# Three attention mixers on TensorE: the value products of the batch before, then the transposes of this batch

## What is computed

```python
s = jnp.einsum('bqhd,bkhd->bhqk', qb, k) * scale
q_pos = i * Q_BLOCK + jnp.arange(Q_BLOCK)
p = masked_softmax(s, key_pos[None, :] <= q_pos[:, None])
return jnp.einsum('bhqk,bkhd->bqhd', p.astype(v.dtype), v)
```

## Time and profile before

| what | us |
|---|---|
| median of 3 executions | 2275.53 |
| lowest and highest of them | 2273.96 and 2278.75 |
| the profiled execution | 2274.43 |
| its span, first to last instruction | 2272.6 |
| of it PE busy | 2130.4 (94%) |
| first attention, about | 152 to 176 |
| MLA's attention, about | 1478 to 1503 |
| NSA's attention, about | 1990 to 2057 |

### The profile page before, as it was taken

One profiled execution on the slowest core, in us unless ns is written; L12 is line 12 of the kernel. 1 busy time (PEld: TensorE's weight loads), 2 busy tenths in 40 slices (PEclk: granted clock), 3 DMA queues, 4 the chain that ended last, 5 costly groups with the idle time before them and its releaser, 6 DMA issues.

```text
span 2272.6 us, 26953 instructions
## 1 busy us (share of the span) xinstructions
PE 2130.4 (94%) x10954; PEld 1282.6 (56%) x10954; DVE 1031.1 (45%) x1712; ACT 673.4 (30%) x1055; POOL 25.4 (1%) x38
## 2 busy tenths in 40 slices
PE   5999899998999899899968999999999999989998
PEld 3348743333333234333315887778888886567887
DVE  7986712222222122222216555765555553375555
ACT  3144311111011011001004444564444442165443
POOL 0000000000000000000000000100000000200000
PEclk8999899999999999999988999999999999989999
DMA  7773799999999999999996452344553443313441
GB/s 317 295 279 125 275 408 426 427 428 427 427 426 428 428 427 427 428 427 426 426 426 258 178 210 92 149 167 167 206 211 139 184 186 116 148 57 137 196 180 70
DMA packets 43506, 633.83 MB, mean 279 GB/s; under 512 B 5104, under 2 KB 5104, under 8 KB 6288
## 3 DMA queue, kind: packets, MB, share of 16 engines
q1 hardware_dynamic: 43376, 632.04, 67.7%
HBM read 630.97 MB, written 1.05 MB: 278 GB/s over the span
## 4 chain that ended last, share of the span: by engine, by line
PE 73%; DMA 15%; DVE 7%; ACT 3%; issue 2%; SPq 0%; ACTq 0%; DVEq 0%
DMA piece<-in_moe 15%; PE bank L2407 13%; PE bank L2302 12%; PE bank L2304 12%; PE bank L2303 12%; PE bank L2448 6%; PE bank L643 3%; PE bank L2388 2%; PE bank L2472 2%; PE bank L1059 1%; PE bank L2748 1%; PE bank L2784 1%; ACT ffn_hi L2909 1%; PE bank L1235 1%; DVE ffn_lo L2308 1%
## 5 line engine op out<-in xcount | busy, mean ns | idle before, releaser
L2407 PE MATMUL bank<-piece,xeT 128*64 128x512 f32 (+1 forms) x2304 | 447.9, 620 | 50.5 <-DMA piece<-in_moe 42.6
L2308 DVE TENSOR_TENSOR ffn_lo<-slot,ffn_hi 128x2048 fp32r<-128x2048 f32 x132 | 302.0, 2291 | 153.2 <-ACT ffn_hi L2909 147.6
L2407 PEld LDWEIGHTS bank<-piece,xeT 128*64 128x64 f32 (+1 forms) x2304 | 135.0, 131 | 330.1 <-issue 307.0
L2909 ACT ACTIVATE ffn_hi<-slot 128x2048 fp32r<-128x2048 f32 x132 | 251.8, 1913 | 126.3 <-PE bank L2304 115.9
L2302 PE MATMUL bank<-ffn_hi,hT_hi 128*128 128x512 f32 x672 | 265.4, 395 | 2.8 <-DVE ffn_lo L2308 2.8
L2304 PE MATMUL bank<-ffn_hi,hT_lo 128*128 128x512 f32 x672 | 261.9, 390 | 0.0
L2303 PE MATMUL bank<-ffn_lo,hT_hi 128*128 128x512 f32 x672 | 261.4, 389 | 0.0
L2527 DVE TENSOR_TENSOR hT<-hT,bank 128x512 f32<-128x512 f32 x144 | 92.1, 681 | 258.4 <-PE bank L2472 258.3
L2575 DVE TENSOR_SCALAR work<-bank 128x256 f32<-128x256 f32 x60 | 25.5, 424 | 336.3 <-PE bank L2416 336.3
L2302 PEld LDWEIGHTS bank<-ffn_hi,hT_hi 128*128 128x128 f32 x672 | 126.2, 188 | 28.5 <-issue 3.6
L2304 PEld LDWEIGHTS bank<-ffn_hi,hT_lo 128*128 128x128 f32 x672 | 126.1, 188 | 26.9
(11 more groups left out here) (724 smaller groups left out, 2723.4 us busy)
## 6 DMA issues: line engine op xcount, KB each, us to landing
piece<-in_moe SPq DMA_DIRECT2D x190, 2048.0 KB, 26.4
slot<-in_ffn SPq DMA_DIRECT2D x44, 3072.0 KB, 10.3
slot<-in_ada SPq DMA_DIRECT2D x16, 1024.0 KB, 5.5
slot<-in_nsa_in SPq DMA_DIRECT2D x5, 2048.0 KB, 7.4
slot<-in_merge SPq DMA_DIRECT2D x3, 3072.0 KB, 11.8
slot<-in_ada SPq DMA_DIRECT2D x2, 3072.0 KB, 18.5
slot<-in_w_in SPq DMA_DIRECT2D x6, 1024.0 KB, 7.7
slot<-in_hy_in SPq DMA_DIRECT2D x3, 2048.0 KB, 7.7
```

Of the source, the lines that this page charges most:

```text
L2308: return dve.tensor_tensor(lo, x, hi.bitcast(F32), ALU.subtract)
L2407: mm = pe.matmul(bank[n * c:n * (c + 1), :], x[:, kt, :], w[i][:, at:at + 512], start=kt == 0, stop=False)
L2909: act.activation(k["ffn_hi"][:, ffn_room(m, piece), :], k["ring"][it.slot][:, piece * PIECE:(piece + 1) * PIECE], ACT.Copy).then_inc(s["ff ...
```

## The change

In the loop of `attend_tensor`, the value products of batch n-1 stand ahead of the transposes of batch n. The same instructions are issued, with the same waits, and no other engine's list is altered.

```diff
         if ("turn", n) in fill:
             fill["turn", n]()
-        turn(u)
         if n >= 1:
             weigh(batches[n - 1])
+        turn(u)
         if after is not None and n in after:
             after[n]()
```

## The result

| | before | after |
|---|---|---|
| median of 7 executions each on one chip, us | 2274.63 | 2283.53 |
| lowest and highest | 2273.14 and 2278.75 | 2281.40 and 2288.75 |
| ratio of the times, 95% interval | | 1.0042, 1.0032 to 1.0051 |
| the profiled execution (span) | 2274.43 (2272.6) | 2281.40 (2279.6) |

The kernel became 8.9 us slower (0.4%). Predicted were 2286.6 us, measured were 2283.53: inside the range, and slower as predicted.

A forecast was written before the change was run, and what follows sets the result against it. Each attention was taken as close to PE-bound with small waits. NSA +9.8, clock +1.1, first attention -0.6 and MLA +0.8 sum to +11.1 us, a median of 2286.6; own range 2282 to 2291, 8-in-10 range 2281 to 2298.

The forecast's parts named there:

- The ring: NSA: scores S, value products W, transposes T, ACT copy C, S again; 7.75 us per two batches instead of 6.29.
- T to C: Start of a batch's transposes to start of the ACT copy of the banks they wrote, 0.91 us.
- C to S: Start of that ACT copy to start of the scores that need it, 0.88 us.
- Five pairs and two hand-overs: NSA: scores 5 to 15, five pairs of batches, +7.3 us; scores 3 to 4 and 4 to 5, 0.99 each, +2.0.
- The tail: NSA, from scores 15 to the first output product: 8.38 us instead of 7.89, +0.5.
- The clock: NSA's start: the new gap delays the clock's rise, half a batch taken, +1.1 us (bounds 0 and +4.4).
- The first attention: The last batch's value products move earlier, to when `out` leaves the shared bank, -0.6 us (bounds -0.8 and 0).
- MLA: Transposes of batch 1 and the work behind them come later, delaying the first output products, +0.8 us (bounds 0.2 and 0.9).
- What follows: After NSA: PE waits only once more, 0.7 us, so at most 0.7 of NSA's loss is hidden.
- Faster: Rival: value products fill the wait for `p_norm`, PE runs its own 5.77 us per pair; about 2272.3 us, chance 0.04.
- Hardly any change: Rival: the ring costs under 0.35 us per batch more; about 2279 us, chance 0.08.
- The low clock: Rival: NSA's clock falls back or stays low; half the time +14 us (2299), all +28 (2313); chance 0.13.

The follow-up runs named there:

- e11: NSA alone: value products of batch n-1 put ahead of the scores of batch n+2, against the kernel before; 2284.39 us beside 2275.05, ratio 1.0055.
- e3: NSA alone: value products split, two ahead of the transposes, the rest and the compressed product behind, against the kernel before; 2278.41 us beside 2275.69, ratio 1.0015.
- e4: Order of e1 plus one extra unused ACT copy ahead of each NSA copy of transposed probabilities; 2288.45 us beside 2274.64 of the kernel before, ratio 1.0060.
- e8: New order in NSA plus 34 unused filler products in PE's four waits at NSA's start; 2282.55 us, ratio to the kernel before 1.0035.
- e7: Order of before plus 34 unused filler products in PE's four waits at NSA's start; 2273.38 us beside 2274.64 of the kernel before, ratio 0.9992.
- e1: New order in NSA alone, the other two attentions as before; 2283.88 us beside 2275.69 of the kernel before, ratio 1.0044.
- e6: New order in the first attention only, NSA's compressed product moved behind the first branch's value products; 2275.08 us beside 2275.69 of the kernel before, ratio 0.9998.
- e2: New order in the first attention and MLA alone, NSA as before; 2274.39 us, ratio to the kernel before 0.9997.
- e10: e9 with fewer fillers, 6, 3, 5 and 3 in place of 12, 5, 12 and 5; 2269.90 us beside 2275.05 of the kernel before, ratio 0.9980.
- e9: e6 plus the 34 filler products of e7; 2271.35 us beside 2274.64 of the kernel before, ratio 0.9988.

## Why the prediction was right, point by point

**The ring (right).** Predicted were T to C 0.91, C to S 0.88, S to W 0.97, W 0.80 or 1.43, 7.75 us for a pair; the trace has 0.91, 0.86, 0.98 and 7.72. That steps of the old order could be put together into an order that no trace had shown worked because the latencies taken were true ones: both rows carried a wait in them. e11 moves the pair as the ring says, e3 and e4 do so within 0.21 and 0.13 us.

**Five pairs and two hand-overs (right, the hand-overs a little large).** The five pairs lost 7.14 us for 7.3. The two hand-overs lost 0.80 and 0.95 at a clock of 1.00 (e8 against e7) for 0.99 each. They had been read from a stretch that was for the most part at 0.50, where the W behind T takes 1.48 us and covers the copy whole; so the old order had no wait there to give up, and in e1, at 0.50 too, S(3) to S(4) took 5.72 us for 4.75, 0.97 more. At 1.00 that W takes 0.80, and the old order has a small wait of its own: S(3) to S(4) took 2.75 us in e7, where S, T and W are 2.57.

**The tail (+0.5, measured +0.29).** The steps held (W waits 0.90 for the copy twice). Mis-sized was the last one: from T(15) to the first output product PE took 0.63 us (2057.99 to 2058.62), not the 0.80 that T to W takes.

**The clock (+1.1, the term that failed).** I took half a batch, on the thought that the new gap would delay the clock's rise. The traces show no such link. At NSA's start the clock read 0.50 for 13.5 us in before, for about 7 us in two pieces in after, 17 us in e1 (new order) and 17 us in e6 (old order, with the compressed product moved), 3.5 us in e3. It varies from one execution to the next by more than the term: after and e1 have the same list in NSA, and from S(0) to S(5) they took 20.39 and 23.40 us. The after trace gained from it: NSA lengthened by 7.5 us there and not by 9.2. MLA lost some 1.6 us to a low clock in the same trace (12.53 us for the 10.95 of e2), so the two nearly cancelled there by luck. What sets the stretch is open.

**The first attention (-0.6, measured -0.57) and MLA (+0.8, measured +0.65 in e2).** Right, and for the reasons given: W(3) waits for `out` and no longer for PE's W(2), and MLA's first output product waits 0.61 for DVE's low part where it waited 0.17.

**What follows.** PE's one wait behind NSA is still 0.7 us, and from NSA's first output product to the end of the span it took 220.96 us before and 220.98 after. So nothing was given back, as the earlier trace rows said:

```profile
PE bank L2302 <- DVE ffn_lo L2308: 0.7, 1, 0.7
```

**The sum.** The forecast was 3.1 us too high. 0.9 of it is the base: before had a median of 2274.63 in the runs beside after, not 2275.53. 1.1 is the clock term, for which no run shows a cost of the order, and 0.6 is NSA's at an even clock (9.8 for 9.17). The remaining 0.5 is below what these medians tell.

**The rivals.** *Faster* fell: S waits 0.90 us for the copy in each batch; the wait for `p_norm` that W was to fill was 0.24 per pair. *Hardly any change* fell: the cost is 0.71 per batch, not under 0.35. *The low clock* fell: over NSA's last 51.50 us PE was busy 38.90 us, 76%, with a gap in each batch, and the granted clock was 1.00, the 2.4 GHz level. The Trainium skill ("TensorE: Matmul & The Clock Gate", section "A second HAM failure mode: psum-queue depth-cycling") describes a bf16 kernel whose clock oscillates when PE cycles through PSUM banks and idles briefly between groups; this ring does both, and in these 51.50 us the trace doesn't agree with it.

## What to carry to other kernels

Between an instruction that starts a hand-over to another engine and the one that needs its result, keep enough work of the first engine to cover the whole round trip (here 1.77 us, of which the transposes themselves cover 0.80); the work is best from another batch. Before moving such work to fill a wait, compare the two: here a wait of 0.24 us per pair of batches was filled by uncovering 0.97 per batch. A short loop can come out either way: of the two with four batches, the first attention gained 0.57 us and MLA lost 0.65, by what waits behind each. So choose the order per loop.

## What the runs showed of the hardware that I had not expected

The low clock at NSA's start goes away when PE is given work in its waits there. All four kernels with fillers (e7 to e10) read 1.00 over the whole of NSA in their profiled executions, and all nine without read 0.50 for some stretch. Whether the same holds in the executions without a profile is not shown. In e10 some 4.6 us of fillers were enough, with waits of 0.2 to 1.1 us left between them. Why the clock falls there in some executions for longer than in others stays open.

A float32 product of 128x128 by 128x128 stands in the trace as two instructions, as the four products of each S stand as eight: 12 of them are 24 in e7's trace and took 2.94 us, 0.245 each, while six transposes of the same size take 0.80. In e7 to e9 the fillers were therefore longer than the waits that they filled (S(0) to S(3) 12.31 us, in e10 10.86).
